# Up projection of a gated MLP: one more pair of column blocks computed by seven half products

## The chip, the cores and the metric

The kernel runs on one core of a Trainium2 chip. The metric is the device time of one execution in microseconds (us), as the median of three runs. TensorE (PE) does the matrix products, VectorE (DVE), ScalarE (ACT) and GpSimd (POOL) the elementwise work, and SyncE (SP) issues most of the transfers.

## What is computed

One decoder layer on 1024 tokens of width 1024. A mixing part (gated DeltaNet, sparse attention, Conformer convolution) comes first and is not touched. Then comes the MLP, and the change lies in its first product:

```
def conv_gated_mlp(x, w_up, conv_w, w_down):
    h = causal_dwconv(x @ w_up, conv_w)
    gt, val = jnp.split(h, 2, axis=-1)
    return (jax.nn.silu(gt) * val) @ w_down
```

`w_up` is 1024 x 5632, so there are 22 pairs of column blocks: pair j is block j of the 128-wide gate columns and block j of the value columns. The convolution has 3 taps along the tokens.

## The kernel before, in words

Every float32 operand of a matmul is split into a high and a low part (`_p` and `_q`). For a weight, ACT makes the high part (`h`, L1993, 128x512) and POOL the low part (`l`, L2000, 128x512); a product is two matmuls, high by high and low by low, with scale factors that make the two add up. The activations `h2_p` and `h2_q` (1024 tokens, K in two halves) are split once.

**Three ways to compute a pair.** Pairs 0 to 2 are done unit by unit (`up_products`, L1798; slots `up_p`, `up_q`, letters U, L, D in the order). Pairs 3 and 4 are "classic" (kind `c`): four weight slabs A1, A2, B1, B2 (gate or value columns, first or second half of K), 16 matmuls of 512 tokens each, 64 in all (L2182). Pairs 5 to 21 are of kind `s`: Strassen's scheme in Winograd's form, seven half products of 8 matmuls each, 56 in all (L2176). Products 1, 2 and 3 take `h2` itself; products 5, 6, 7 and 4 take the four tiles t5, t6, t7, t4, which are sums of quarters of `h2`.

**What seven products want beside PE.** Per pair: 4 sums of weight slabs on DVE (`s`, L2123, 128x512, both inputs in SBUF), 3 additions to PSUM on DVE (`a`, L2130), 3 copies out of PSUM on ACT (`k`, L2057), and 7 splits in place of 4 on ACT and POOL. Once for all pairs, DVE makes the t tiles: `W` (L2092, 128x2048) takes a quarter of `h2` whole, `S` (L2101) subtracts, ACT splits (`H`, L2045), DVE takes the low part (`T`, L2105). T7 overwrites the place of two of the sums, so it comes after T6 and T4.

**Behind every pair**, whichever way it was computed: ACT multiplies by tap 2 (`t`, L2015), DVE adds taps 1 and 0 (`c`, L2078, and `v`, L2084, each reading PSUM), ACT takes silu (`y`, L2049), and the product of the two blocks (`p`) is made by POOL for pairs 0 to 2 (L2069) and by DVE for the others (L2140). In the order, `v1.2` is tap 0 of the value columns (1) of pair 2, and `s6.5` the sum for product 6 of pair 5.

**What sets the order.** PE takes the products in the order of the list MULTS, from `up_order()`: pair by pair, product 1 of an `s` pair two places ahead of the end of the `s` pair before it. The other queues take their steps in the order of the table UP_ORDER, written out as words; `up_run` (L1860) gives each engine the words that it owns. The slabs lie in a ring of five (RING), so the split of product n waits for product n-5.

PSUM holds the results of two pairs at a time. PE waits before a product until the taps have read what lies there:

```
                if i in (1, B1):
                    conv_done(pe, 1, j - 2)
                if i in (2, 5, A1):
                    conv_done(pe, 0, j - 2)
                if j < CLASSIC + 2 and i in (1, 2, 5, A1, B1):
                    conv_done(pe, 1, j - 2)
```

Before the first product of pair 3 PE so waits for `v0.1` and `v1.1`, and before that of pair 4 for `v0.2` and `v1.2`.

**The start of the down projection** (L2388) reuses slab places: the load of its second weight block (`e1`) waits for the last product in ring place 3, and the split of that block (`f1`) for the last in ring place 4 (`dn_load`, `dn_split_hi`). PE needs that block after the first 8 matmuls of the down projection. The first block's place is free earlier.

Of the kernel before, what the change touches and what calls it, by code (L numbers as in the profile page):

```python
# [170 lines left out]
def key_blocks(t, kind):  # L171
    return (0, t + 1) if kind == 0 else win_blocks(t)
# [84 lines left out]

CLASSIC = 3
RING = 5
UP_KINDS = "ccsssssssssssssssss"  # L260
SEVEN = [j for j in range(CLASSIC, NF) if UP_KINDS[j - CLASSIC] == "s"]
A1, A2, B1, B2 = "a1", "a2", "b1", "b2"


def up_order():
# [15 lines left out]


UP_ORDER = (
# [29 lines left out]
)  # L313
UP_STEPS = [(x[0],) + tuple(int(y) if y.isdigit() else y for y in x[1:].split(".")) for x in UP_ORDER.split()]

# [76 lines left out]
def build(nc, a, out, scratch, qkv_mid, act_mid):  # L392
    ctx = ExitStack()
    with ctx:
# [7 lines left out]
        def late(name, value=0):  # L402

            early, base = LATE[name]
            return sem(early), base + value
# [396 lines left out]
        for t, kind, _ in GROUPS:  # L802
            k0, k1 = key_blocks(t, kind)
# [988 lines left out]
        def up_products(pe, u, halves, ks=range(KD)):  # L1792

            j, g = divmod(u, 2)
            for k in ks:
                for w, x in ((up_p[up_slot(u)], h2_p), (up_q[up_slot(u)], h2_q)):
                    for h in halves:
                        ins = pe.matmul(up_ps[j % 2][:, g, h * 512:(h + 1) * 512], w[:, k], x[:, h, k],  # L1798
                                        start=k == 0 and x is h2_p, stop=True, skip_group_check=True)
            return ins  # L1800
# [58 lines left out]
        def part_done(eng, i, j):  # L1859

            eng.wait_ge(*late("up_lo", 3 + LOWS.index(("l", i, j)) + 1))
# [17 lines left out]
        def t_ready(eng, i):  # L1879
            eng.wait_ge(*late("t_lo", T_LOS.index((i,)) + 1))  # L1880
# [7 lines left out]
        def conv_done(eng, g, j):  # L1888
            eng.wait_ge(*late("up_conv", CONVS.index((g, j)) + 1))
# [4 lines left out]
        def copy_done(eng, i, j):  # L1894
            eng.wait_ge(*late("c_cp", U_COPIES.index((i, j)) + 1))
# [253 lines left out]
        def up_pe(pe):  # L2149
            pe.wait_ge(*late("v_lo", NT))  # L2150
            for u in range(2 * CLASSIC):
                pe.wait_ge(*late("up_lo", u + 1 if u < 3 else 3 + LOWS.index(("L", u)) + 1))
                if u >= 4:
                    conv_done(pe, u % 2, (u - 4) // 2)
                up_products(pe, u, (1,) if u < 3 else (0, 1)).then_inc(late("up_mm")[0], 1)

            for n, (i, j) in enumerate(MULTS):
                part_done(pe, i, j)
                if i in (1, B1):
                    conv_done(pe, 1, j - 2)  # L2160
                if i in (2, 5, A1):
                    conv_done(pe, 0, j - 2)
                if j < CLASSIC + 2 and i in (1, 2, 5, A1, B1):
                    conv_done(pe, 1, j - 2)
                if i in t_p:
                    t_ready(pe, i)
                if i in (6, 7):
                    copy_done(pe, {6: 1, 7: 6}[i], j)
                if i == 4:
                    copy_done(pe, 7, j)  # L2170
                if i == 3:
                    add_done(pe, 5, j)
                for k in range(HT):
                    if j in SEVEN:
                        for w, x in ((slab_p[n % RING], x_p[i]), (slab_q[n % RING], x_q[i])):
                            ins = pe.matmul(mult_ps(i, j), w[:, k], x[:, k], start=k == 0 and x is x_p[i] and i in (1, 2, 5),  # L2176
                                            stop=True, skip_group_check=True)
                    else:
                        g, kh = divmod((A1, A2, B1, B2).index(i), 2)
                        for w, h in ((slab_p[n % RING], h2_p), (slab_q[n % RING], h2_q)):  # L2180
                            for th, part in enumerate((left, right)):
                                ins = pe.matmul(c_ps(g, j)[:, part], w[:, k], x_quad(h, kh, th)[:, k],  # L2182
                                                start=k == 0 and h is h2_p and kh == 0, stop=True, skip_group_check=True)
                ins.then_inc(late("up_mm")[0], 1)
# [857 lines left out]
```

## Time and profile before

| | us |
|---|---|
| median of 3 runs | 1161.19 (1160.9 to 1163.57) |
| the profiled execution | 1163.38 |
| its span, first to last instruction | 1161.6 |
| PE busy | 1113.5 (96%) |
| DVE, ACT, POOL busy | 861.3, 636.8, 444.9 |
| granted TensorE clock, mean | 0.995 |

Busy times are sums of the instructions' spans. Matmuls are pipelined: each is shown for some 0.39 us, and the next one starts before that has passed. An instruction of DVE or POOL that waits for something inside the engine is shown as longer, and not as idle time before it. Beside idle time stands what ended it.

### The profile page before, as it was taken

The page shows a single profiled execution, that of the slowest core. Times are in us where ns is not written, and L with a number is a line of the kernel's source. Part 1 is how long each engine was busy: PE and PEld are TensorE (multiplying, and loading weights), DVE is VectorE, ACT ScalarE, POOL GpSimd, SP SyncE. Part 2 cuts the span into 40 slices and gives each one's busy share as a digit, 9 for nine tenths or more (in the row PEclk, how much of TensorE's full clock was granted, in tenths as well). Part 3 has the DMA queues.
Part 4 walks back from the last instruction along what each step waited for, and adds up shares of the span by engine and source line. Part 5 has one row for each costly group of instructions (what it writes and reads, how often), then busy time and mean ns, then how long its engine had stood idle before and what let it go on. Part 6 is the DMA issues. An engine that isn't in the chain of part 4 may idle for free.

```text
span 1161.6 us, 23435 instructions
## 1 busy us (share of the span) xinstructions
PE 1113.5 (96%) x9394; PEld 917.3 (79%) x9394; DVE 861.3 (74%) x1132; ACT 636.8 (55%) x1199; POOL 444.9 (38%) x449
## 2 busy tenths in 40 slices
PE   5999999999999999999997999999999999999997
PEld 5878879878878778878776887788888777788886
DVE  5798976656668785767654758979989999755755
ACT  7544333447565545464565755466667667545543
POOL 2477346222122131220214024768878888100000
PEclk9999999999999999999998999999999999999999
DMA  8345210510000000000106334233343334875771
GB/s 260 91 111 169 80 44 19 112 44 23 3 22 22 2 23 2 23 2 3 38 2 199 128 128 129 70 91 127 112 143 109 118 118 128 303 281 185 274 278 73
DMA packets 111858, 118.76 MB, mean 102 GB/s; under 512 B 16276, under 2 KB 90248, under 8 KB 111752
## 3 DMA queue, kind: packets, MB, share of 16 engines
q1 hardware_dynamic: 110312, 112.03, 30.8%
q10 hardware_dynamic: 1440, 5.24, 1.1%
q8 instruction: 76, 1.25, 0.4%
q14 instruction: 30, 0.25, 0.1%
HBM read 94.68 MB, written 22.54 MB: 101 GB/s over the span
## 4 chain that ended last, share of the span: by engine, by line
PE 74%; DVE 14%; ACT 3%; POOL 3%; issue 3%; DMA 2%; SPq 0%; DVEq 0%; ACTq 0%
PE psum L2388 13%; PE psum L2176 10%; PE psum L1445 8%; PE psum L2964 7%; PE psum L1692 5%; PE psum L1625 4%; PE psum L3004 4%; PE psum L1641 4%; DVE arena L2849 3%; PE psum L1798 3%; POOL slab_q L2000 3%; PE psum L1606 2%; PE psum L2182 2%; DVE arena L2078 1%; PE psum L1438 1%
## 5 line engine op out<-in xcount | busy, mean ns | idle before, releaser
L2000 POOL TENSOR_TENSOR slab_q<-arena,slab_p 128x512 fp32r<-128x512 f32 x127 | 206.4, 1654 | 45.6 <-ACT slab_p L1993 45.4
L1445 PE MATMUL psum<-arena 64*64 64x64 f32 x3072 | 110.8, 221 | 2.7 <-DVE arena L1221 1.5
L2388 PE MATMUL psum<-dn_p,ap_p 128*128 128x512 f32 x352 | 110.2, 392 | 3.2 <-DVE ap_q L2253 2.9
L1445 PEld LDWEIGHTS psum<-arena 64*64 64x64 f32 x3072 | 97.5, 134 | 17.9 <-issue 6.8
L2388 PE MATMUL psum<-dn_q,ap_q 128*128 128x512 f32 x352 | 109.8, 391 | 0.0
L2176 PE MATMUL psum<-t_p,slab_p 128*128 128x512 f32 x272 | 106.3, 391 | 1.2 <-ACT arena L2057 0.8
L2176 PE MATMUL psum<-t_q,slab_q 128*128 128x512 f32 x272 | 105.9, 389 | 0.0
L1993 ACT ACTIVATE slab_p<-arena 128x512 fp32r<-128x512 f32 x127 | 78.1, 627 | 35.7 <-PE psum L2176 13.3
L1127 ACT ACTIVATE arena<-psum 128x384 f32<-128x384 f32 x132 | 60.3, 489 | 59.6 <-PE psum L1625 59.0
L2214 DVE TENSOR_TENSOR dn_q<-arena,dn_p 128x1024 fp32r<-128x1024 f32 x41 | 50.2, 1224 | 56.3 <-ACT dn_p L2204 56.2
L1329 DVE TENSOR_REDUCE arena<-psum 128x1 f32<-128x640 f32 (+7 forms) x96 | 66.9, 705 | 32.2 <-PE psum L1610 30.4
L2964 PE MATMUL psum<-h_p,cm_p 128*128 128x512 f32 (+1 forms) x288 | 87.4, 375 | 0.5 <-DVE arena L2871 0.5
L2964 PE MATMUL psum<-h_q,cm_q 128*128 128x512 f32 (+1 forms) x288 | 86.8, 373 | 0.0
L1120 ACT ACTIVATE arena<-psum,arena 128x640 f32<-128x640 f32 (+7 forms) x96 | 67.0, 700 | 35.0 <-DVE arena L1329 34.3
L2204 ACT ACTIVATE dn_p<-arena 128x1024 fp32r<-128x1024 f32 x44 | 46.6, 1058 | 70.0 <-PE psum L2388 64.9
L2176 PE MATMUL psum<-h_p,slab_p 128*128 128x512 f32 x204 | 79.8, 391 | 1.0 <-POOL slab_q L2000 1.0
L2388 PEld LDWEIGHTS psum<-dn_p,ap_p 128*128 128x128 f32 x352 | 65.8, 188 | 19.0 <-POOL dn_q L2214 2.8
L2176 PE MATMUL psum<-h_q,slab_q 128*128 128x512 f32 x204 | 79.4, 389 | 0.0
L2388 PEld LDWEIGHTS psum<-dn_q,ap_q 128*128 128x128 f32 x352 | 66.1, 188 | 14.6
L2849 DVE SCALAR_TENSOR_TENSOR arena<-psum,arena 128x1023 f32<-128x1023 f32 (+29 forms) x60 | 75.9, 1264 | 1.4
L2123 DVE TENSOR_TENSOR arena<-arena 128x512 f32<-128x512 f32 x68 | 72.8, 1085 | 0.0
L986 POOL TENSOR_TENSOR arena<-arena 128x384 f32<-128x384 f32 x16 | 16.0, 999 | 131.8 <-DVE arena L1295 71.2
(326 smaller groups left out, 2726.1 us busy)
## 6 DMA issues: line engine op xcount, KB each, us to landing
arena<-in_ffn_w_up SPq DMA_DIRECT2D x44, 512.0 KB, 5.2
arena<-in_ffn_w_down SPq DMA_DIRECT2D x44, 512.0 KB, 4.2
arena<-in_w_in SPq DMA_DIRECT2D x20, 512.0 KB, 3.8
act_mid<-arena SPq DMA_DIRECT2D x18, 512.0 KB, 2.6
arena<-act_mid SPq DMA_DIRECT2D x36, 256.0 KB, 5.1
arena<-in_x SPq DMA_DIRECT2D x16, 512.0 KB, 5.6
qkv_mid<-arena ACTq DMA_DIRECT2D x9, 512.0 KB
arena<-qkv_mid SPq DMA_DIRECT2D x8, 576.0 KB, 4.3
```

The lines of the kernel that those rows point to most:

```text
L1120: act.activation(probs(u), s_psum(u, n), ACT.Exp, bias=nmx[:, u % 2:u % 2 + 1], accum_out=psums[:, NH * kind + h:NH * kind + h + 1]).then_ ...
L1127: act.activation(pt[x % 2].rearrange("p g c -> p (g c)"), psum[:, bank, 0:GDIM], ACT.Copy).then_inc(done, 1)
L1329: v.tensor_reduce(nmx[:, u % 2:u % 2 + 1], s_psum(u, n), AX.X, ALU.max, negate=True).then_inc(sem("n_mx"), 1)
L1445: ins = pe.matmul(out[rows, h * CH:(h + 1) * CH], lhs[rows, h], rhs[rows, h], start=start, stop=True, skip_group_check=True)
L1692: ins = pe.matmul(wm_ps[WM_SLOT[t]][:, n * 512:(n + 1) * 512], x[:, k], w[:, n * 512:(n + 1) * 512], start=first and k == ks[0] and w is w ...
L1993: act.activation(slab_p[n % RING], part_source(i, j), ACT.Copy, scale=1.0 - SPLIT_W).then_inc(late("up_hi")[0], 1)
L2000: pool.tensor_tensor(slab_q[n % RING], part_source(i, j), slab_p[n % RING], ALU.subtract).then_inc(late("up_lo")[0], 1)
L2123: v.tensor_tensor(out, x, y, op).then_inc(late("s_add")[0], 1)
L2176: ins = pe.matmul(mult_ps(i, j), w[:, k], x[:, k], start=k == 0 and x is x_p[i] and i in (1, 2, 5), stop=True, skip_group_check=True)
L2388: ins = pe.matmul(dn_ps[t % HT][:, n * 512:(n + 1) * 512], x[:, tok], w[:, n * 512:(n + 1) * 512], start=first and x is ap_p[s], stop=True ...
L2849: own.up(v.scalar_tensor_tensor(out=cacc[:, c, s:S], in0=glu[c][:, 0:S - s], scalar=w, in1=cacc[:, c, s:S], op0=ALU.mult, op1=ALU.add))
L2964: ins = pe.matmul(cm_ps[i % 2][:, c0:c1], w[:, k], x[:, k, c0:c1], start=k == 0 and x is h_p, stop=True, skip_group_check=True)
```

## The change

The letter of pair 4 in UP_KINDS goes from `c` to `s`, so that 18 pairs are computed by seven products. MULTS then holds 4 + 18 x 7 = 130 products in place of 8 + 17 x 7 = 127. The table UP_ORDER is replaced as a whole; its first line stands in the diff. PE waits for one tap more (`conv_done(pe, 0, j - 2)`) in pairs 3 and 4.

```diff
-UP_KINDS = "ccsssssssssssssssss"
+UP_KINDS = "cssssssssssssssssss"
...
-    "D3 D4 D5 W5 d3 t0.0 U3 c0.0 U4 L3 W7 ha1.3 t1.0 L4 v0.0 U5 W6 la1.3 t0.1 y0 L5 c1.0 c0.1 v1.0 S5 p0 t1.1 d4 c1.1 H5 S7 hb2.3 T5 "
+    "D3 D4 D5 W5 d3 t0.0 U3 c0.0 U4 L3 W7 ha1.3 t1.0 L4 v0.0 U5 c1.0 la1.3 t0.1 W6 y0 L5 v1.0 S5 p0 t1.1 d4 c0.1 H5 S7 c1.1 hb2.3 T5 "
...
                 if j < CLASSIC + 2 and i in (1, 2, 5, A1, B1):
+                    conv_done(pe, 0, j - 2)
                     conv_done(pe, 1, j - 2)
```

Place 1, DVE ahead of the first product of pair 3. L2101 is `S`, L2105 with `t_q5` is T5, L2078 is a `c`, and "L2084 x2" is the pair of taps v0.1 and v1.1. Before:

```order
L2078 SCALAR_TENSOR_TENSOR arena<-psum,arena 128x1023
L2101 TENSOR_TENSOR arena<-arena 128x2048
L2105 SCALAR_TENSOR_TENSOR t_q5_164<-t_p5_160,arena 128x2048
L2084 SCALAR_TENSOR_TENSOR arena<-psum,arena 128x1022 x2
L2101 TENSOR_TENSOR arena<-arena 128x2048
```

After the change:

```order
L2101 TENSOR_TENSOR arena<-arena 128x2048
L2078 SCALAR_TENSOR_TENSOR arena<-psum,arena 128x1023
L2105 SCALAR_TENSOR_TENSOR t_q5_164<-t_p5_160,arena 128x2048
L2101 TENSOR_TENSOR arena<-arena 128x2048
L2084 SCALAR_TENSOR_TENSOR arena<-psum,arena 128x1022 x2
```

The third `S` (S6) now stands ahead of the two taps v0.1 and v1.1, where it stood behind them.

Place 2, DVE from those taps to the last tap of pair 2. L2092 is W4, L2101 is S4, t_q6, t_q4 and t_q7 are T6, T4 and T7, L2123 is a weight sum. Before:

```order
L2084 SCALAR_TENSOR_TENSOR arena<-psum,arena 128x1022 x2
L2101 TENSOR_TENSOR arena<-arena 128x2048
L2092 SCALAR_TENSOR_TENSOR arena<-h2_p_132,h2_q_133 128x2048
L2078 SCALAR_TENSOR_TENSOR arena<-psum,arena 128x1023 x2
L2101 TENSOR_TENSOR arena<-arena 128x2048
L2084 SCALAR_TENSOR_TENSOR arena<-psum,arena 128x1022 x2
L2105 SCALAR_TENSOR_TENSOR t_q6_165<-t_p6_161,arena 128x2048
L2105 SCALAR_TENSOR_TENSOR t_q4_167<-t_p4_163,arena 128x2048
```

After the change:

```order
L2092 SCALAR_TENSOR_TENSOR arena<-h2_p_132,h2_q_133 128x2048
L2105 SCALAR_TENSOR_TENSOR t_q6_165<-t_p6_161,arena 128x2048
L2101 TENSOR_TENSOR arena<-arena 128x2048
L2078 SCALAR_TENSOR_TENSOR arena<-psum,arena 128x1023
L2123 TENSOR_TENSOR arena<-arena 128x512
L2105 SCALAR_TENSOR_TENSOR t_q4_167<-t_p4_163,arena 128x2048
L2084 SCALAR_TENSOR_TENSOR arena<-psum,arena 128x1022
L2078 SCALAR_TENSOR_TENSOR arena<-psum,arena 128x1023
L2123 TENSOR_TENSOR arena<-arena 128x512
L2084 SCALAR_TENSOR_TENSOR arena<-psum,arena 128x1022
L2105 SCALAR_TENSOR_TENSOR t_q7_166<-t_p7_162,arena 128x2048
```

T6, T4 and two weight sums of pair 4 (s5.4 and s6.4) now stand ahead of v0.2, the last of the two L2084; T6 and T4 stood behind both taps of pair 2.

Place 3, POOL from its split l1.4 on (L2000; the number of `slab_q` is the ring place, L2069 is p1 or p2). Before:

```order
L2000 TENSOR_TENSOR slab_q4_177<-arena,slab_p4_172 128x512
L2069 TENSOR_TENSOR arena<-arena 128x1024
L2000 TENSOR_TENSOR slab_q1_174<-arena,slab_p1_169 128x512
L2000 TENSOR_TENSOR slab_q2_175<-arena,slab_p2_170 128x512
L2000 TENSOR_TENSOR slab_q0_173<-arena,slab_p0_168 128x512
```

After the change:

```order
L2000 TENSOR_TENSOR slab_q4_177<-arena,slab_p4_172 128x512
L2000 TENSOR_TENSOR slab_q1_174<-arena,slab_p1_169 128x512
L2000 TENSOR_TENSOR slab_q2_175<-arena,slab_p2_170 128x512
L2069 TENSOR_TENSOR arena<-arena 128x1024
L2000 TENSOR_TENSOR slab_q2_175<-arena,slab_p2_170 128x512
```

The low part of slab A2 of pair 3 (ring place 1) now stands ahead of p1. Later, p2 stands between l1.5 and l7.4.

## Rows read from the trace of the kernel before

**Rows 1.** Page, part 1: busy time and share of the span.

```profile
PE 1113.5 (96%) x9394; PEld 917.3 (79%) x9394; DVE 861.3 (74%) x1132; ACT 636.8 (55%) x1199; POOL 444.9 (38%) x449
```

**Rows 2.** Windows by stage: length, busy us of PE, PEld, DVE, ACT, POOL, clock, DMA.

```profile
738.60:769.30 30.70, 29.55 (x131) 24.14 (x130) 24.35 (x16) 15.91 (x17) 22.58 (x11) 1.00 0.25 69
769.30:989.80 220.50, 218.22 (x954) 177.91 (x953) 211.15 (x202) 151.08 (x224) 184.89 (x118) 1.00 0.39 121
989.80:1000.70 10.90, 8.06 (x34) 5.69 (x32) 9.44 (x8) 4.63 (x5) 3.66 (x2) 1.00 0.93 324
1000.70:1161.60 160.90, 154.29 (x672) 126.00 (x672) 93.08 (x100) 76.72 (x116) 2.35 (x1) 1.00 0.65 228
```

**Rows 3.** Line L2182, classic pairs: duration min/median/max, first and last start.

```profile
L2182 PE MATMUL psum<-h_p,slab_p x64: 387/389/496, 738.8 to 768.6; 128*128 128x512 f32 x64
```

**Rows 4.** PE's timeline, 741 to 745 us: start, length, instruction, idle time before.

```profile
741.99 0.61 PE L2182 MATMUL psum<-h_q,slab_q 128*128 128x512 f32 x2
743.75 0.72 PE L2182 MATMUL psum<-h_p,slab_p 128*128 128x512 f32 x2 [1.15 <-POOL slab_q L2000]
```

**Rows 5.** DVE's timeline, 717 to 761 us.

```profile
717.88 3.30 DVE L2092 SCALAR_TENSOR_TENSOR arena<-h_p,h_q 128x2048 f32<-128x2048 f32 x1
...
731.29 2.28 DVE L2105 SCALAR_TENSOR_TENSOR t_q<-t_p,arena 128x2048 fp32r<-128x2048 f32 x1
733.50 2.46 DVE L2084 SCALAR_TENSOR_TENSOR arena<-psum,arena 128x1022 f32<-128x1022 f32 x2
735.88 2.27 DVE L2101 TENSOR_TENSOR arena<-arena 128x2048 f32<-128x2048 f32 x1
738.08 4.48 DVE L2092 SCALAR_TENSOR_TENSOR arena<-h_p,h_q 128x2048 f32<-128x2048 f32 x1
...
747.06 2.46 DVE L2084 SCALAR_TENSOR_TENSOR arena<-psum,arena 128x1022 f32<-128x1022 f32 x2
749.45 4.64 DVE L2105 SCALAR_TENSOR_TENSOR t_q<-t_p,arena 128x2048 fp32r<-128x2048 f32 x2
...
760.04 0.68 DVE L2123 TENSOR_TENSOR arena<-arena 128x512 f32<-128x512 f32 x1
```

**Rows 6.** POOL's timeline, 714 to 759 us.

```profile
714.82 4.21 POOL L1970 TENSOR_TENSOR up_q<-arena,up_p 128x1024 fp32r<-128x1024 f32 x1 [0.20 <-ACT up_p L1966]
718.99 3.35 POOL L2000 TENSOR_TENSOR slab_q<-arena,slab_p 128x512 fp32r<-128x512 f32 x1
...
755.20 2.40 POOL L2069 TENSOR_TENSOR arena<-arena 128x1024 f32<-128x1024 f32 x1
757.55 1.29 POOL L2000 TENSOR_TENSOR slab_q<-arena,slab_p 128x512 fp32r<-128x512 f32 x1
```

**Rows 7.** ACT's timeline, 726 to 733 us.

```profile
726.99 1.92 ACT L2045 ACTIVATE t_p<-arena 128x2048 fp32r<-128x2048 f32 x1 [1.36 <-DVE arena L2101]
731.76 1.16 ACT L1993 ACTIVATE slab_p<-arena 128x512 fp32r<-128x512 f32 x2 [2.85 <-PE psum L1798]
```

**Rows 8.** Groups of instructions from 769.3 to 989.8 us: busy, mean ns, idle before.

```profile
L2000 POOL TENSOR_TENSOR slab_q<-arena,slab_p 128x512 fp32r<-128x512 f32 x116 | 182.4, 1602 | 34.4 <-ACT slab_p L1993 34.4
L2123 DVE TENSOR_TENSOR arena<-arena 128x512 f32<-128x512 f32 x65 | 70.7, 1104 | 0.0
```

**Rows 9.** Start of the down projection: PE's and SP's timelines, landing times, groups.

```profile
989.77 0.63 PE L2388 MATMUL psum<-dn_p,ap_p 128*128 128x512 f32 x2
994.15 0.70 PE L2388 MATMUL psum<-dn_p,ap_p 128*128 128x512 f32 x2 [2.36 <-DVE ap_q L2253]
983.47 0.33 SPq L2258 DMA_DIRECT2D arena<-in_ffn_w_down  x1
DMA to landing us min/median/max: 3.5/4.2/11.6
L2204 ACT ACTIVATE dn_p<-arena 128x1024 fp32r<-128x1024 f32 x44 | 46.6, 1058 | 70.0 <-PE psum L2388 64.9 <-DMA arena<-in_ffn_w_down 5.1
L2214 POOL TENSOR_TENSOR dn_q<-arena,dn_p 128x1024 fp32r<-128x1024 f32 x3 | 7.5, 2503 | 1.4 <-ACT dn_p L2204 1.4
```

56 rows, old and new, of the table UP_ORDER are left out of this document.

## Prediction, made blind

> **What bounds the kernel now.** I read the page's busy times first: PE 96% busy, no other engine above 74% [rows 1]. So a gain must take work or gaps from PE. Next the windows by stage [rows 2], from which the reader should see three things. The classic pairs (738.6 to 769.3) take 30.7 us, and PE is busy for 29.55. The seventeen seven-product pairs take 220.5 us at full clock. After them come 10.9 us in which PE is busy for 8.06, and then an even stretch of 161 us that the change leaves alone. Last the timelines of DVE and POOL before and inside the classic pairs, because there the new work has to fit.
>
> PE's own price: from the first to the last high-part matmul of the classic pairs there are 125 steps in 29.8 us [rows 3], with a gap of 1.3 [rows 4]; so matmuls that follow each other start 0.227 us apart. The 17 x 56 = 952 of the seven-product pairs would take 215.9 us and took 220.5, so 4.6 us are lost there in small waits for slabs. DVE is busy for 211.15 of the 220.5 us, POOL for 184.89 [rows 2].
>
> **DVE and POOL hold each other up.** An S step of DVE (L2101, 128x2048) takes 2.27 us alone, and W4 (L2092), equally large, 4.48 when it starts at 738.08 [rows 5]. POOL's slab split takes 1.29 us [rows 6], but 1.60 on average in the seven-product pairs, and DVE's weight sum 0.68 [rows 5] but 1.10 [rows 8]. One case shows the mechanism: W6 starts at 717.88 while POOL's split from 714.82 runs until 719.03, and lasts 3.30 us, which is 1.15 of waiting and 2.2 of work. POOL's la1.3 starts at 718.99, ends at 722.34, and needs 1.29 alone [rows 5, 6]: it waited until W6 was through. Instructions of DVE with an input in PSUM (taps, 1.2 us each from start to start) keep their length. So W, S, T, s and p on DVE, and everything on POOL, run one after another.
>
> **What is removed.** Pair 4 needs 56 matmuls in place of 64: 8 x 0.227 = **1.8 us less**. The gap at 743.75 [rows 4] (1.76 us from start to start where 0.45 is usual, so 1.3) goes too: there PE waited for the low part of slab A2, which stood behind p1 on POOL and now stands ahead. **1.3 us less.**
>
> **What is added, and where it lands.** DVE gets 4 weight sums and 3 additions, ACT 3 copies and 3 splits, POOL 3 splits. The sizes are small, but DVE has no free time from 717.88 to 754 [rows 5]; its free time lies after that, when pair 4 is already running. I walk the new order with the spacings of these rows: 2.2 us for W, S and T, 1.2 for a tap, 0.6 for a weight sum, 1.29 and 2.40 for POOL, 1.9 for H, 0.6 for a split on ACT [rows 5, 6, 7].
>
> *Gap A, before pair 3.* PE is ready at 738.8 [rows 3] and needs v0.1 and v1.1. Before, they ended at 735.96. Now a tap follows 717.88 and ends at 719.1; POOL has just taken la1.3 (719.0 to 720.3); W6 runs to 722.5; POOL's L5 to 724.9; S5 to 727.1; p0 to 729.5 with c0.1 beside it; S7 to 731.7; c1.1 to 732.9. POOL takes lb2.3, whose high part comes at 731.76 to 732.3 [rows 7], until 733.7; T5 to 735.9; l1.4 to 737.2; S6 to 739.4; both taps to 741.8. Gap about **2.9 us**. If POOL loses la1.3 and lb2.3 to DVE instead, everything comes two POOL splits earlier and the gap is 0.9; a further split ahead of S6 makes it 3.3.
>
> *Gap B, before product 1 of pair 4.* PE would be ready 14.5 us after 741.7, at 756.2, and needs v0.2. DVE from 741.8: W4 behind lb1.3 (742.6) to 744.8; p1 on POOL to 747.2; T6 to 749.4; S4 to 751.6; c1.2, s5.4 to 753.4; T4, waiting for H4 (751.7 to 753.6), to 755.8; v1.2 and c0.2 to 758.2; s6.4 to 759.0 behind l5.4; v0.2 to 760.2. PE starts about 760, so **3.8 us**. Before, these taps ended at 749.5 [rows 5], with T6 and T4 behind them. Bounds 1.5 and 4.3: where POOL takes none of these turns, and where it takes one more.
>
> *Gap C, inside pair 4.* h6.4 on ACT now stands behind the copy k1.4, so it starts when product 1 has ended (762): split at 763.3, low part at 764.6, while product 5 ends at 763.6, so 1.0 us. p2 (2.4 us on POOL, after y2, which waits for v0.2 and h1.5) stands ahead of l7.4: l1.5 to 765.9, p2 to 768.3, l7.4 to 769.6 at best, where PE could start product 7 at 768.2; that is 1.5. Together **2.5 us**; below, nothing (ACT and POOL may catch up), above 3.3.
>
> *The pairs behind.* The 18th pair costs what the others do. After the gaps of 9.2 us, less the 3.1 saved, PE is 6.1 us later than before, while DVE and POOL go on through the gaps and gain a lead. Their lag caused the 4.6 us of waits, so part of these is not waited again: between 0 and 4.6, I take half, **2.3 us less**, since the lead is used up after some pairs.
>
> *Start of the down projection.* With 130 products the last ones in ring places 3 and 4 are the last two of all; with 127 they were the fourth and the third from the end. So the load e1, issued at 983.47, 6.3 us before the first matmul of the down projection [rows 9], now goes out only 1.8 us before it. Landing 4.2, high part 1.06, low part on POOL 2.4 [rows 9, 6]: 5.9 us after that matmul, and PE wants the block after 1.8. A gap of 4.1, against 2.36 before the same matmuls and 1.3 more behind it (10.9 less 2.36 less 32 x 0.227). The later waits were for the taps of pair 21, which end during the new gap. 7.3 + 4.1 = 11.4 against 10.9: **0.5 us more** (0 to 4).
>
> **Sum.** -1.8 - 1.3 + 2.9 + 3.8 + 2.5 - 2.3 + 0.5 = **+4.3 us**. The profiled execution (1163.38; 1.8 around its span) would go to 1167.7. The median lies 2.2 lower, at 1161.19, and goes to **1165.5**. What a measurement here tells from no change is 0.3%, 3.5 us.
>
> **A rule weighed.** Whole instructions wait for each other in the rows, but how much of an instruction's length keeps the other engine out is open, and with it whether POOL and DVE together fill a pair. POOL's seven splits are 7 x 1.29 = 9.0 us. With DVE's full length (0.68 a sum, the product of the blocks as large as two) 4.1 more make 13.1; with its spacing (0.6) 3.6 more make 12.6. PE needs 56 x 0.227 = 12.7 and got 12.97. If it is the 13.1, DVE and POOL set the pace, PE's late arrival is paid back to the full 4.6, and the sum is +2.0. If it is the 12.6, it is +4.3; I keep this, as PE has work in 218.2 of the 220.5 us [rows 2]. The Trainium skill ("SBUF — State Buffer", Who interferes with whom) says that whichever of the two engines issues first holds the shared port pair for the whole instruction, when DVE has two inputs in SBUF. Taken at its word, with the lengths shown, that speaks for +2.0; the trace agrees that they exclude each other (W6 and la1.3 above) and does not show the length held.
>
> **The rivals.**
> - *Pace set by DVE and POOL.* 13.1 us of theirs per pair: +2.0, 1163.2. For: 12.97 us per pair. Against: PE 218.2 of 220.5 busy. Chance 0.18.
> - *The turns fall kindly.* POOL loses the turns at 719 and 732: gaps 0.9, 1.5 and 0.5 in place of 9.2 together, with 1 us repaid: -3.1 + 2.9 - 1 + 0.5 = -0.7, 1160.5. For: before, W6 did win at 717.88. Against: the tap put ahead of it gives POOL that turn. Chance 0.14.
> - *Faster.* The new order of sums and copies in pairs 5 to 21 ends the waits for slabs: all 4.6 us, with gaps as in the kind case: -3.1 + 2.9 - 4.6 + 0.5 = -4.3, 1156.9. It decides if s3 and s5 of the next pair, now side by side, never hold up a split. Against: DVE has just 9 us to spare in 220. Chance 0.06.
> - *Worse.* The new order lets DVE lag once per pair, 0.3 us each over 17 pairs with nothing repaid: +4.3 + 2.3 + 5 = +11.6, 1172.8. Chance 0.07.
> - *As forecast*, +2.5 to +7.5 us, most of it above 3.5: chance 0.55.
>
> **Numbers.** 1165.5. The range 1160.4 to 1169.2 takes in the kind case, the pace case and the forecast up to a little under its upper bounds (+8.0). Slower by over 0.3%: 0.07 and 0.43 of the forecast's 0.55, 0.50. Faster by over 0.3%: the 0.06 and a little of the kind case, 0.08. Within: 0.42.
>
> **What would show it.** After: PE idle of 2 to 3 us just before its first L2182 matmul, released by DVE L2084; 3 to 4 us before the first product of pair 4, by the same line; two smaller gaps within it, for L2000; 56 matmuls fewer by 8; one gap of 4 us at the start of L2388 for POOL L2214, and 11.4 us for that stage. If the taps v0.1 and v1.1 end before PE needs them, the walk is wrong at its first step, and the kernel is no slower.

## The result and the profile after

The kernel after the change takes **1172.03 us** (median of 4 runs, 1170.36 to 1173.76) against 1162.38 for the kernel before in the same comparison (1160.9 to 1163.6, 4 runs): a ratio of 1.008, 95% interval 1.0063 to 1.0097. It is slower by 9.65 us. The forecast was 1165.5, slower by 4.3, with a range from 1160.4 to 1169.2; the sign was right, the size was not. In all code of the changed kernel from L2163 on, line numbers are one higher than before (L2177 for the `s` products, L2183 for the classic ones, L2389 for the down projection).

Page, part 1, and windows by stage of the changed kernel (length, busy us of PE, PEld, DVE, ACT, POOL, clock, DMA), to read against [rows 1] and [rows 2]:

```profile
PE 1116.5 (95%) x9386; PEld 920.1 (79%) x9386; DVE 871.3 (74%) x1139; ACT 637.6 (54%) x1205; POOL 453.6 (39%) x452
```

```profile
740.35:768.82 28.47, 24.80 (x96) 19.91 (x96) 22.98 (x15) 13.10 (x17) 16.75 (x8) 0.88 0.13 37
770.43:996.48 226.05, 223.45 (x976) 182.65 (x977) 218.46 (x209) 149.67 (x226) 194.43 (x121) 1.00 0.38 120
996.48:1010.11 13.63, 10.06 (x33) 7.72 (x32) 11.03 (x11) 8.08 (x9) 4.69 (x2) 0.75 0.81 284
1010.11:1171.00 160.89, 154.20 (x673) 126.01 (x671) 91.46 (x98) 75.26 (x114) 2.35 (x1) 0.99 0.65 230
```

The last stretch is as long as before. The mean clock is 0.88 in the first and 0.75 in the third stretch, where [rows 2] had 1.00 throughout. Where PE waited (its timeline; idle time before an instruction and its releaser stand in brackets):

```profile
740.35 0.70 PE L2183 MATMUL psum<-h_p,slab_p 128*128 128x512 f32 x2 [1.51 <-POOL slab_q L2000]
758.81 0.76 PE L2177 MATMUL psum<-h_p,slab_p 128*128 128x512 f32 x1 [3.67 <-DVE arena L2084]
759.37 0.63 PE L2177 MATMUL psum<-h_q,slab_q 128*128 128x512 f32 x1
759.80 0.63 PE L2177 MATMUL psum<-h_p,slab_p 128*128 128x512 f32 x1
770.43 0.50 PE L2177 MATMUL psum<-t_p,slab_p 128*128 128x512 f32 x1 [1.23 <-POOL slab_q L2000]
1002.08 1.22 PE L2389 MATMUL psum<-dn_p,ap_p 128*128 128x512 f32 x2 [3.57 <-POOL dn_q L2215]
```

These are gap A, gap B, one half of gap C and the gap at the start of the down projection. At gap A the row names POOL's split la2.3, which ended at 740.21, but product A1 of pair 3 wants only la1.3, long done; what it waited for was the tap v1.1, which ended at 740.20 (the rows of DVE below; a kernel with another order of these splits has the same gap and there the row names the tap). Behind gap B matmuls start 0.43 us apart, not 0.227. The windows around the two long gaps show why:

```profile
757.00:759.00 2.00, 0.19 (x1) 0.22 (x2) 2.00 (x3) 0.00 (x0) 0.00 (x0) 0.78 0.00 0
759.00:764.00 5.00, 5.00 (x12) 3.91 (x13) 2.96 (x3) 1.40 (x3) 0.21 (x1) 0.50 0.00 0
766.00:768.00 2.00, 2.00 (x11) 1.64 (x10) 0.74 (x1) 2.00 (x4) 2.00 (x2) 1.00 0.00 0
1000.00:1002.00 2.00, 0.00 (x0) 0.00 (x0) 1.96 (x3) 1.54 (x2) 2.00 (x2) 0.61 0.99 311
1002.00:1006.00 4.00, 3.92 (x9) 3.15 (x10) 2.84 (x3) 1.82 (x2) 2.36 (x2) 0.50 0.86 287
```

In both gaps the granted clock falls from 2.4 to 1.2 GHz (1.00 to 0.50) while PE is idle, and comes back 5 to 6 us after PE has work again. From 758.81 to 764.92 that is 14 matmuls at 0.427 us in place of 0.227, which with the first one's start makes 2.9 us; behind 1002.08 it is 12 more, about 2.4 us. The Trainium skill ("TensorE: Matmul & The Clock Gate", HAM oscillation) describes this pattern, a wait after which the next tile starts at the low clock and a price of half the time spent there; the trace agrees (6.1 us at half speed, 2.9 us lost).

DVE's timeline at the places of [rows 5], which decides gaps A and B:

```profile
732.24 2.28 DVE L2105 SCALAR_TENSOR_TENSOR t_q<-t_p,arena 128x2048 fp32r<-128x2048 f32 x1
734.44 3.38 DVE L2101 TENSOR_TENSOR arena<-arena 128x2048 f32<-128x2048 f32 x1
737.75 2.46 DVE L2084 SCALAR_TENSOR_TENSOR arena<-psum,arena 128x1022 f32<-128x1022 f32 x2
742.33 3.37 DVE L2105 SCALAR_TENSOR_TENSOR t_q<-t_p,arena 128x2048 fp32r<-128x2048 f32 x1
745.62 4.48 DVE L2101 TENSOR_TENSOR arena<-arena 128x2048 f32<-128x2048 f32 x1
752.09 2.29 DVE L2105 SCALAR_TENSOR_TENSOR t_q<-t_p,arena 128x2048 fp32r<-128x2048 f32 x1 [0.19 <-ACT t_p L2045]
756.68 0.68 DVE L2123 TENSOR_TENSOR arena<-arena 128x512 f32<-128x512 f32 x1
757.28 1.28 DVE L2084 SCALAR_TENSOR_TENSOR arena<-psum,arena 128x1022 f32<-128x1022 f32 x1
```

v0.1 and v1.1 now end at 740.2, where they ended at 735.96; T6, S4, T4 and s6.4 stand ahead of v0.2, which ends at 758.56, 0.25 us before PE starts. And SP's timeline of the changed kernel has the late load `e1`, 1.6 us ahead of the first matmul of the down projection at 996.48 (6.3 in [rows 9]):

```profile
994.85 0.33 SPq L2259 DMA_DIRECT2D arena<-in_ffn_w_down  x1
```

**The ledger.** What lies before the up projection varied by up to 3.5 us between the executions, so times are counted from one fixed instruction: the matmul of the first three pairs (L1798) that waits 0.54 us for `h_q`, at 706.00 before and 705.87 after. From there to the end of the span the kernel took 455.6 us before and 465.1 after, +9.5:

| part | forecast | measured |
|---|---|---|
| 8 matmuls less in pair 4 | -1.8 | -1.8 |
| the wait at 743.75 [rows 4] | -1.3 | -1.3 |
| gap A | +2.9 | +1.7 |
| gap B, its length | +3.8 | +3.8 |
| slow clock behind gap B | none | +2.9 |
| gap C | +2.5 | +1.4 |
| paid back in the pairs behind | -2.3 | +0.1 |
| start of the down projection | +0.5 | +2.7 |
| sum | +4.3 | +9.5 |

The steady pairs: 976 matmuls of 0.2268 us are 221.4 us and took 226.05, so 4.7 are lost where 4.6 were. The down projection's start took 13.63 us for 10.9. The ledger is that of one execution: its mean clock was 0.988, and that of the kernel's other three executions 0.989 to 0.992, so the slow stretches may well be shorter in most.

### The profile page after: what moved, and what is told of

The parts are those of the page before. It is cut to its first block, busy times and chain, and to the rows that moved or that the text cites. A ratio compares the mean times of both kernels' runs of the same rounds, so it can differ in the third digit from the quotient of the medians.

```text
span 1171.0 us, 23458 instructions
## 1 busy us (share of the span) xinstructions
PE 1116.5 (95%) x9386; PEld 920.1 (79%) x9386; DVE 871.3 (74%) x1139; ACT 637.6 (54%) x1205; POOL 453.6 (39%) x452
## 4 chain that ended last, share of the span: by engine, by line
PE 76%; DVE 13%; ACT 4%; issue 3%; DMA 2%; POOL 2%; SPq 0%; DVEq 0%; ACTq 0%; POOLq 0%
PE psum L2177 17%; PE psum L2389 14%; PE psum L1445 8%; PE psum L2965 7%; PE psum L1692 5%; PE psum L1625 4%; PE psum L3005 4%; PE psum L1641 4%; DVE arena L2850 3%; PE psum L1606 2%; PE psum L1438 1%; DVE arena L2101 1%; DMA arena<-in_ffn_w_up 1%; DVE arena L2084 1%; PE psum L1390 1%
## 5 line engine op out<-in xcount | busy, mean ns | idle before, releaser
L2000 POOL TENSOR_TENSOR slab_q<-arena,slab_p 128x512 fp32r<-128x512 f32 x130 | 213.0, 1663 | 43.5 <-ACT slab_p L1993 43.0
L2177 PE MATMUL psum<-t_p,slab_p 128*128 128x512 f32 x288 | 113.8, 395 | 3.8 <-ACT arena L2057 2.6
L2389 PE MATMUL psum<-dn_p,ap_p 128*128 128x512 f32 x352 | 111.5, 397 | 4.0 <-POOL dn_q L2215 3.6
L2177 PE MATMUL psum<-t_q,slab_q 128*128 128x512 f32 x288 | 113.1, 393 | 0.0
L2389 PE MATMUL psum<-dn_q,ap_q 128*128 128x512 f32 x352 | 111.0, 395 | 0.0
L2215 DVE TENSOR_TENSOR dn_q<-arena,dn_p 128x1024 fp32r<-128x1024 f32 x41 | 50.2, 1225 | 58.9 <-ACT dn_p L2205 58.9
L2177 PE MATMUL psum<-h_p,slab_p 128*128 128x512 f32 x216 | 85.2, 394 | 3.7 <-DVE arena L2084 3.7
L2205 ACT ACTIVATE dn_p<-arena 128x1024 fp32r<-128x1024 f32 x44 | 46.6, 1059 | 74.3 <-PE psum L2389 70.3
L2177 PE MATMUL psum<-h_q,slab_q 128*128 128x512 f32 x216 | 85.1, 394 | 0.0
L2123 DVE TENSOR_TENSOR arena<-arena 128x512 f32<-128x512 f32 x72 | 83.8, 1184 | 0.0
L2389 PEld LDWEIGHTS psum<-dn_p,ap_p 128*128 128x128 f32 x352 | 66.9, 191 | 19.3 <-POOL dn_q L2215 4.0
L2389 PEld LDWEIGHTS psum<-dn_q,ap_q 128*128 128x128 f32 x352 | 67.0, 190 | 14.8
L2177 PEld LDWEIGHTS psum<-t_p,slab_p 128*128 128x128 f32 x288 | 54.6, 190 | 18.7 <-POOL slab_q L2000 6.1
```

Of the source, the lines that this page charges most:

```text
L2000: pool.tensor_tensor(slab_q[n % RING], part_source(i, j), slab_p[n % RING], ALU.subtract).then_inc(late("up_lo")[0], 1)
L2123: v.tensor_tensor(out, x, y, op).then_inc(late("s_add")[0], 1)
L2389: ins = pe.matmul(dn_ps[t % HT][:, n * 512:(n + 1) * 512], x[:, tok], w[:, n * 512:(n + 1) * 512], start=first and x is ap_p[s], stop=True ...
```

## The experiments

A line more or less in a kernel moves the line numbers behind it: the products by seven are L2176, L2177, L2178 or L2181, the classic ones L2182 or L2184, the copy `k` L2056 or L2057, the tap `v` L2083 or L2084, the weight sum L2122 or L2123, the slab split L1999 or L2000, the down projection L2388, L2390 or L2393. All ratios are against the kernel before, whose median was 1163.01 us in both series of runs (11 and 17).

**Is the slow clock due to the gap?** The kernel after (from here on the filler kernel), with PE given 14 matmuls in gap B that nobody needs (their results lie in a place that is overwritten before it is read):

```diff
+                if (i, j) == (1, CLASSIC + 1):
+                    conv_done(pe, 1, j - 2)
+                    for _ in range(14):
+                        pe.matmul(mult_ps(5, j), slab_p[n % RING][:, 0], x_p[1][:, 0], start=True, stop=True, skip_group_check=True)
```

> The changed kernel with 14 matmuls that nobody reads, put into PE's gap ahead of product 1 of pair 4, as soon as the other half of that PSUM bank group is free (v1.2). The work of the kernel and its output stay. Theory 1 (the fall of the granted clock after that gap costs time of its own): in the changed kernel's trace the next 14 matmuls start 0.43 us apart in place of 0.227, 2.9 us; with the filler the clock stays at 1.00 there, the first product of pair 4 still starts at 758.8, and the time falls by 1.8 to 2.9 us (the waits for slabs behind it may take back up to 1.1), to 1169.1 to 1170.2. Rival (the slow stretch hides waits that would come anyway, for DVE and POOL): the clock stays at 1.00, but products 7 or 5 of the next pairs wait 3 us longer, and the time stays at 1172.0.

Measured 1171.47 us (1168.38 to 1172.68, 4 runs), ratio 1.0072 (1.0046 to 1.0098). Windows of this kernel, columns as above, and its two waits inside pair 4:

```profile
757.00:759.00 2.00, 2.00 (x10) 1.67 (x9) 2.00 (x3) 0.65 (x2) 0.00 (x0) 1.00 0.00 0
759.00:764.00 5.00, 4.25 (x19) 3.17 (x19) 1.81 (x3) 4.96 (x8) 4.46 (x3) 1.00 0.00 0
1001.00:1004.00 3.00, 3.00 (x9) 2.37 (x8) 1.84 (x3) 1.30 (x2) 1.72 (x1) 0.54 0.86 270
760.87 0.50 PE L2181 MATMUL psum<-t_p,slab_p 128*128 128x512 f32 x1 [0.75 <-POOL slab_q L2000]
766.17 0.50 PE L2181 MATMUL psum<-t_p,slab_p 128*128 128x512 f32 x1 [1.37 <-POOL slab_q L2000]
```

With PE busy through the gap the clock stays at 1.00: the fall belongs to the gap. Product 7 of pair 4 was reached 1.6 us earlier, not 2.9, since part of the slow stretch had hidden waits for the splits: at full clock gap C is 2.6 us (the two waits and the slow starts behind them), close to the 2.5 forecast, and not 1.4. The rival had that much right. And the total shows nothing of the 1.6 us: about 200 us behind the fixed instruction, one pair's weights land late, and PE waits 2.37 us (about 1 in the kernel after). In the steady pairs ACT waited 3.7 us in three places for `arena<-in_ffn_w_up` (0.7 in one place in the kernel after, never in the kernel before). At the down projection the gap (3.40 us) and the slow clock are there again. What is shown is thus the effect on the clock and 1.6 us within pair 4; a gain in the median is not.

**Is lateness paid back?** Two kernels that are the kernel before, with one wait added in front of slab product A1 of pair 4, for p2 (short) or for the tap t0.3 (long):

```diff
+                if (i, j) == (A1, CLASSIC + 1):
+                    prod_done(pe, 2)
```

```diff
+                if (i, j) == (A1, CLASSIC + 1):
+                    pe.wait_ge(*late("up_tap", TAPS_UP.index((0, CLASSIC)) + 1))
```

> The kernel before with one wait more: product A1 of pair 4 waits on PE for p2 of POOL (ended at 757.6), a gap of 3.5 us where there was none, and nothing else changed. Theory 1: what decides is the length of the gap; at 3.5 us it is between 2.5 (no fall seen) and 3.8 us (fall seen). With a fall +3.5 +2.9 = +6.4 us, without it +3.5, less what the pairs behind pay back. Rival (the late arrival of PE is paid back, since DVE and POOL gain a lead): at least 2 of these us come back in pairs 5 to 21, whose stretch takes 218.5 us in place of 220.5. If nothing is paid back: 1165.9 or 1168.8.

> The kernel before with one wait more: product A1 of pair 4 waits for tap t0.3 of ACT (ended at 758.8), a gap of 4.7 us. Theory 1: the clock falls to half for some 6 us after it, 14 matmuls at 0.43 us: +4.7 +2.9 = +7.6 us, 1170.0. Without a clock effect: +4.7, 1167.1. With payback in the pairs behind: up to 4.6 us less in either case.

Measured: short 1168.01 us (1165.72 to 1170.42, 7 runs), ratio 1.0043 (1.0026 to 1.006); long 1170.54 (1167.6 to 1171.41, 5 runs), ratio 1.0058 (1.0037 to 1.008). PE's timeline and the windows of the short one, with the steady pairs and the down projection behind ("issue": no releaser is seen):

```profile
756.95 0.57 PE L2184 MATMUL psum<-h_p,slab_p 128*128 128x512 f32 x1 [2.69 <-issue]
757.00:759.00 2.00, 2.00 (x5) 1.56 (x6) 0.91 (x1) 2.00 (x2) 1.09 (x1) 0.54 1.14 330
773.16:993.70 220.54, 218.18 (x953) 177.83 (x952) 211.23 (x202) 151.08 (x224) 184.97 (x118) 1.00 0.39 121
998.15 0.47 PE L2390 MATMUL psum<-dn_p,ap_p 128*128 128x512 f32 x1 [2.37 <-DVE ap_q L2255]
998.00:1001.00 3.00, 2.85 (x9) 2.07 (x10) 3.00 (x4) 0.00 (x0) 0.00 (x0) 0.75 0.84 298
```

The same of the long one:

```profile
756.77 0.77 PE L2184 MATMUL psum<-h_p,slab_p 128*128 128x512 f32 x1 [3.91 <-POOL slab_q L2000]
772.83:993.40 220.57, 218.19 (x953) 177.85 (x952) 210.28 (x202) 151.02 (x224) 185.06 (x118) 1.00 0.39 121
```

PE came to pair 5 4.6 us late in the one and 5.6 in the other, and the seventeen pairs took 220.54 and 220.57 us where [rows 2] has 220.50. Nothing is paid back. The chain of waits of PE says why there was nothing to repay. Kernel before and short gap, waits of PE for POOL from 771 to 989 us (sum, times, longest):

```profile
PE psum L2176 <- POOL slab_q L2000: 1.4, 6, 0.5
```

```profile
PE psum L2178 <- POOL slab_q L2000: 1.5, 6, 0.5
```

The same six waits, as long as before, though DVE and POOL had been given 4.6 us. They do not lag; the products that they wait for themselves (a slot of the ring, a result in PSUM) hold them to PE, and the whole pattern shifts with it. From 775 to 989 us ACT waits for PE for 47.1 us before and 46.6 in the short kernel, POOL for ACT's high parts for 32.3 and 34.1. A gap of 2.69 us was enough for the slow clock, at a price of 1.7 us, and that of 3.91 us had a price of 1.5; a later one of 2.37 us had it too, though the kernel before has a gap of 2.36 there at full clock [rows 2, 9].

**The start of the down projection.** The kernel after (from here on the repaired kernel, `tail_ring` in the expectations), with the weight ring's places renumbered so that the two places which the down projection's second block takes over (1 and 2 now) belong to the fourth and the third product from the end, as in the kernel before, and with the words at the end of the order in the turn they had before. Two things went with the new places: at the start ha2.3, hb1.3 and t0.2 of ACT come ahead of hb2.3 and h1.4, and la2.3 and lb1.3 of POOL ahead of lb2.3 and l1.4; and the waits that guard the first splits into the ring changed places with them. So this kernel differs from the kernel after at the start too:

```diff
-        slab_at = (23552, 24576, 25600, 31744, 32768)
+        slab_at = (23552, 31744, 32768, 24576, 25600)
...
-                    sp.wait_ge(*late("up_mm", 2 * CLASSIC + max(n for n in range(PRODUCTS) if n % RING == 3) + 1))
+                    sp.wait_ge(*late("up_mm", 2 * CLASSIC + max(n for n in range(PRODUCTS) if n % RING == 1) + 1))
...
-            act.wait_ge(*late("up_mm", 2 * CLASSIC + max(n for n in range(PRODUCTS) if n % RING == 4) + 1))
+            act.wait_ge(*late("up_mm", 2 * CLASSIC + max(n for n in range(PRODUCTS) if n % RING == 2) + 1))
```

> The changed kernel with its ring places renumbered, so that the last two products of the up projection lie in places that the down projection's second block does not use, and with the order of the steps of pairs 20 and 21 on DVE, ACT, POOL and SP as before. The load e1 and the split f1 then wait for the fourth and third product from the end, as before. Theory 2 (the late load made the 4 us gap, and the gap the fall of the clock): the gap at the start of the down projection shrinks to 2.4 us, the clock stays at 1.00, and that stage takes 10.9 us in place of 13.6: -2.7 us, 1169.3. Rival (the gap is there because DVE is late with pair 21): the stage stays at 13 us or the gap moves into the last pair, 1171 to 1172.

Measured 1171.05 us (1169.36 to 1172.54, 4 runs), ratio 1.0077 (1.0051 to 1.0103). From the reference to the end +7.8 against the kernel before, where the kernel after had +9.5. SP's and PE's timelines:

```profile
757.12 0.76 PE L2176 MATMUL psum<-h_p,slab_p 128*128 128x512 f32 x1 [3.71 <-DVE arena L2083]
760.12 0.39 PE L2176 MATMUL psum<-h_q,slab_q 128*128 128x512 f32 x1
908.07 0.47 PE L2176 MATMUL psum<-t_p,slab_p 128*128 128x512 f32 x1 [2.20 <-ACT arena L2056]
989.35 0.33 SPq L2258 DMA_DIRECT2D arena<-in_ffn_w_down  x1
1000.16 0.70 PE L2388 MATMUL psum<-dn_p,ap_p 128*128 128x512 f32 x2 [2.47 <-DVE ap_q L2253]
```

`e1` goes out 6.3 us before the down projection and the gap is the old one, released by the old instruction. The clock stays at 1.00, and that stage takes 11.0 us again: 2.6 us won. Gaps A and B are as long as in the kernel after (1.52 and 3.71 us). But the slow clock behind gap B covers 7 matmuls here and not 14 (757.12 to 760.12), 1.4 us lost and not 2.9, and the two waits of gap C show in full again (0.74 and 1.38 us), so only 0.4 us are won in pair 4. In the steady pairs 1.2 are lost, by a wait of 2.20 us in one of them (the same pair as in the filler kernel).

**Does the fifth pair cost, or the order?** The fifth pair is pair 4. Three kernels with other orders of words. In the first, only the start differs from the kernel just shown, from the first words to those of pair 4. DVE's words there (behind them T7 follows in the new order, s3.4 in the old):

```diff
-W5 c0.0 W7 v0.0 c1.0 W6 v1.0 S5 c0.1 S7 c1.1 T5 S6 v0.1 v1.1 W4 T6 S4 c1.2 s5.4 T4 v1.2 c0.2 s6.4 v0.2 T7 s7.4
+W5 W7 S5 c0.0 W6 v0.0 c1.0 S7 c0.1 v1.0 S6 c1.1 v0.1 T5 v1.1 W4 c0.2 s5.4 S4 s6.4 T6 v0.2 T4 s7.4 c1.2 v1.2 s3.4
```

In ACT's order h5.4 then stands ahead of t1.2 and h1.4, in POOL's la2.3 and p1 stand ahead of lb1.3, and l5.4 ahead of l1.4.

> The kernel tail_ring with another order of the first words only: on the three engines that make sums and halves, the words up to the last one of pair 4 stand so that pair 4's sums s5.4 and s6.4, their halves h5.4 and h6.4 and the taps of units 0 to 2 come ahead of T6, S4 and T4; all behind keeps the order of tail_ring. Theory 1 (the loss lies in the two gaps at the start, of 1.5 and 3.7 us, and in the slow matmuls behind the second): both gaps go, the granted clock stays at 1.00 through the first pair by seven products, the up stage begins its steady pairs some 7 us earlier than tail_ring, and the time is 1161 to 1165 us. Theory 2 (the fifth pair's added work on VectorE, ScalarE and GpSimd is what costs, in whatever order it stands): the wait only moves to another of the first pairs, and the time stays at 1168 to 1172 us.

Measured **1161.49 us** (1158.37 to 1164.14, 12 runs) against 1163.01 for the kernel before (17 runs), ratio 0.9988 (0.9975 to 1.0), so no slower than the kernel before and hardly to be told from it. Windows by stage, and what was left in the steady pairs:

```profile
737.49:751.95 14.46, 14.46 (x65) 11.98 (x64) 14.43 (x10) 8.39 (x9) 9.03 (x5) 1.00 0.26 72
751.95:987.10 235.15, 230.68 (x1011) 188.57 (x1010) 225.63 (x213) 157.77 (x238) 203.14 (x126) 1.00 0.38 118
987.10:998.11 11.01, 8.01 (x33) 5.66 (x32) 9.59 (x8) 4.60 (x5) 3.79 (x2) 1.00 0.90 309
```

```profile
899.44 0.47 PE L2176 MATMUL psum<-t_p,slab_p 128*128 128x512 f32 x1 [2.60 <-ACT arena L2056]
897.24 0.63 ACT L1992 ACTIVATE slab_p<-arena 128x512 fp32r<-128x512 f32 x1 [2.30 <-DMA arena<-in_ffn_w_up]
```

PE is busy without a break through pair 3 (14.46 us for 64 matmuls) and the clock is at 1.00 in every stage. With the same work in another order the median is 9.6 us lower than in the kernel just shown, and the trace 9.1 from the fixed instruction. Theory 2 of this expectation falls: DVE, ACT and POOL have room for what pair 4 asks. The wait in one steady pair is seen whole here: the copy that PE needs stands on ACT behind a split whose weights have not landed.

In the second the order of all DVE, ACT and POOL words was searched for the whole up projection, with the durations of these traces; SP's order is untouched. In the third the same was done with the 17 pairs of the kernel before.

> All 18 pairs by seven half products as in the change, with the order of VectorE's, ScalarE's and GpSimd's words made anew over the whole up projection so that no product waits by the durations of this case's traces, SyncE's order and the slots as in tail_ring. Theory 1 (order, not the amount of work): no gap over 1 us from the first product to the end of the up stage and none over 1.5 us at the start of the down projection, clock 1.00 throughout, 1150 to 1158 us, faster than the kernel before by 4 to 11 us. Theory 2 (the fifth pair costs in whatever order): not under 1165 us. The weights' lateness (theory 4) would show as ScalarE waiting on loads, and then the gain is 2 us smaller.

> The kernel before, 17 pairs by seven half products, with the order of VectorE's, ScalarE's and GpSimd's words made anew in the same way. If the fifth pair is worth its 8 matmuls of 0.227 us and nothing else once the order is good, opt17 is 1.8 us slower than opt18 (1152 to 1160 us). Rival: the fifth pair costs more than it saves, and opt17 is the faster of the two by 2 us or more.

Measured: 18 pairs **1153.69 us** (1152.24 to 1155.68, 5 runs), ratio 0.9923 (0.9908 to 0.9937). 17 pairs 1156.26 us (1154.76 to 1158.75, 6 runs), ratio 0.9946 (0.9932 to 0.996). Windows of the 18 pairs:

```profile
737.60:752.06 14.46, 14.46 (x65) 11.97 (x64) 14.43 (x10) 8.39 (x9) 9.02 (x5) 1.00 0.27 73
752.06:982.10 230.04, 229.26 (x1009) 188.66 (x1008) 206.19 (x214) 157.25 (x237) 181.25 (x125) 1.00 0.39 122
982.10:992.50 10.40, 9.35 (x40) 7.03 (x39) 8.47 (x8) 7.09 (x8) 4.80 (x2) 1.00 0.82 300
```

and all that PE waited for in it from 771 to 989 us (sum, times, longest):

```profile
PE psum L2388 <- POOL dn_q L2214: 1.0, 1, 1.0
PE psum L2176 <- ACT arena L2056: 0.8, 1, 0.8
```

The last row of these windows holds 40 matmuls where the others hold 33; the first 33 took 8.9 us. The 1008 matmuls are 228.6 us at 0.2268 and took 230.04: 1.4 us are lost, where the kernel before lost 4.6 in 952, and the kernel with the new start alone 6.5 in its 1008. From the fixed instruction to the end the kernel takes 447.2 us, 8.5 less than the kernel before: 1.8 for the 8 matmuls, 1.3 for the wait at 743.75, 3.3 in the steady pairs, and 2.0 at the start of the down projection, where PE's longest wait is now 0.98 us. How that comes about can be read in the groups, kernel after and then this one, both from 769 to 985 us:

```profile
L2123 DVE TENSOR_TENSOR arena<-arena 128x512 f32<-128x512 f32 x68 | 81.2, 1214 | 0.0
L2000 POOL TENSOR_TENSOR slab_q<-arena,slab_p 128x512 fp32r<-128x512 f32 x118 | 189.5, 1631 | 28.0 <-ACT slab_p L1993 27.5
```

```profile
L2122 DVE TENSOR_TENSOR arena<-arena 128x512 f32<-128x512 f32 x65 | 56.9, 899 | 0.7 <-POOL slab_q L1999 0.5
L1999 POOL TENSOR_TENSOR slab_q<-arena,slab_p 128x512 fp32r<-128x512 f32 x115 | 164.1, 1456 | 44.7 <-ACT slab_p L1992 44.5
```

A weight sum shows 0.90 us where it showed 1.21, a slab split 1.46 where it showed 1.63: the same work in another order, which fits two engines that meet less often. With good orders, the fifth pair by seven products is worth 2.6 us by the medians (1156.26 less 1153.69) and 2.3 by the traces, of which 1.8 are its 8 matmuls; the rest is within what is left open, as the two intervals (0.9908 to 0.9937, 0.9932 to 0.996) just overlap. The version with 18 pairs beats both given kernels, by 9.3 and about 18 us.

## Why the prediction failed

Two steps failed: a gap on PE was priced by its length, without the slow clock behind it, and 2.3 us were to be paid back where nothing is. Step by step:

- **What bounds the kernel, and PE's price**: right. The 8 matmuls and the wait at 743.75 came as summed.
- **DVE and POOL hold each other up, and the walk of the new order**: right in kind. Gap B was forecast at 3.8 us with v0.2 as its releaser, and came so to a tenth, though POOL's turns fell differently: T6 waited behind lb1.3 and S4 behind p1. Gap A was 1.7, not 2.9: S6 was through at 737.8, where 739.4 was walked, as l1.4 came behind it on POOL; the releaser was the tap, as forecast. Gap C was 1.4, not 2.5: PE reached that place so slowly that its first half was hidden, and at full clock (filler kernel) it is 2.6.
- **The term that was missing**: gaps were priced by their length alone. The clock's fall behind gap B (2.9 us in this execution, of which some 1.2 hid a part of gap C) stands nowhere in the sum, although the gap itself was right. The prediction gives no reason for leaving it out. In its rows the only gap near in length is that of 2.36 us in [rows 9], in a stretch at 1.00 [rows 2]. But the same trace holds a longer one that it did not read, in the mixing part (PE's timeline and a window of the kernel before):

```profile
624.62 0.90 PE L1390 MATMUL psum<-arena 128*128 128x128 f32 x3 [3.98 <-DVE arena L1261]
625.00:628.00 3.00, 3.00 (x10) 2.42 (x9) 1.84 (x4) 1.49 (x2) 0.00 (x0) 0.50 0.84 206
```

Behind this gap of 3.98 us the 128x512 matmuls start 0.43 us apart. The price of gap B and of the gap at the down projection could have been taken from there.
- **"Start of the down projection", +0.5**: the cause was right (`e1` late, POOL L2215 as releaser, gap 3.57 for a forecast 4.1, and the later waits gone with it), the stage took 13.6 and not 11.4 us. The same missing term again, about 2.4 us: in the repaired kernel gap, slow clock and 2.6 us go together.
- **"The pairs behind", -2.3**: wrong in kind. It took the steady pairs' 4.6 us for a lag that a lead of DVE and POOL could work off. With a delay of 4.6 and of 5.6 us nothing was repaid. At full clock the measured terms would add up to some +5.4 by my estimate (gap C at 2.6, nothing for the clock, 0.3 at the down projection): near the forecast, but partly by luck, since gap A was 1.2 too high and the repayment 2.4 too low. It also answers the rule weighed there: whatever length the port is held for, the pace-setter case (+2.0) would have repaid all of it, and the runs show none. That rival falls.
- **The rivals.** The "worse" one had the right size (1172.8) by a wrong mechanism, a lag per pair of 0.3 us: 4.7 us lost against 4.6 shows no such lag. The "faster" one assumed that an order of the steady pairs could end all their waits. For this change's order it was wrong, but the searched order shows that the room was there; "just 9 us to spare" on DVE counted its waiting for POOL as work.

Not settled: the late weights of one steady pair. All four kernels with the change's steady order have the wait at the same pair, and no other kernel has it. In the filler kernel ACT is ready for these weights 4.9 us after SP issued their load (897.23, ready at 902.13) and gets them at 904.20; the split starts 5.6 us after the issue in the kernel after, 6.8 and 7.2 in the repaired kernel and the one with the new start. So the order asks for this load sooner than its landing allows in these traces; no kernel moved that load by itself, and why the landing varies is open. Also open is why the same gap B was followed by a slow stretch of 6.1 us in one execution and of 2.8 in another.

## What to carry to other kernels

A gap on TensorE has two prices, its length and what the clock takes behind it; in this kernel a gap of 3.7 us was followed by slow matmuls that took 1.4 to 2.9 us more, of which part hid waits that would have come anyway. Before counting on a stretch to pay a delay back, ask whether the engines that are to catch up wait for the delayed one themselves: here they did, and a delay at the start arrived at the end whole. And when work is added to queues that are written out by hand, judge the work and the order apart: the same 18 pairs took 1171, 1161 and 1154 us in three orders.

## What the runs showed of the hardware

- In the up projection and the start of the down projection, the clock fell to half with each of PE's longest gaps (2.69, 3.40, 3.57, 3.67, 3.71, 3.91 us). With eight others of 2.20 to 2.60 us it fell twice, both at the start of the down projection in the kernels with an added wait (2.35 and 2.37), and not in the same place in three other kernels (2.36, 2.47, 2.51). So the same gap in the same place may cost nothing, or some 0.7 us: what the short kernel has more at its end (+5.3) than at the down projection (+4.7). The wait before L1390, in the mixing part, is 3.7 to 4.9 us long in all nine traces, and each time PE starts behind it at 1.2 GHz. Behind the gaps of 2.69, 3.40, 2.35 and 2.37 us PE's first matmuls still ran at full clock or close to it (0.31 to 0.37 us from the first to the second start, where 0.56 to 0.59 is seen when the clock fell inside the gap).
- The price is not fixed either: 2.9 us behind gap B in the kernel after, 1.4 behind the same gap in the kernel with the repaired start of the down projection (3.67 and 3.71 us long), 1.5 behind the gap of 3.91 us and 1.7 behind that of 2.69. The slow matmuls were 14, 7, 7 and 9. Other waits in that stretch were hidden by it, so that keeping the clock up won less (1.6 us) than the slow matmuls cost.
- DVE's and POOL's busy time depends on the order of steps: 871.3 and 453.6 us in the kernel after, 848.1 and 429.1 with the same instructions in the searched order.
